# Final sums and output norm moved into the last two experts of a mixture-of-experts step, on one core

## The reference, cut to what matters

```python
h = x + mix                                     # mixer: pooling, gated linear attention, w_out
hn = rmsnorm(h, norm_ffn)
# router: the best of 4 groups, then the best 2 of its 8 experts; gates = p_group * softmax over the two
def expert_block(xb, e):                        # for the rows sent to expert e
    hid = silu(xb @ w_eg[e]) * (xb @ w_eu[e])   # 1024 -> 512
    return hid @ w_ed[e]                        # 512 -> 1024
h = h + gate1 * y(expert1) + gate2 * y(expert2)
y = rmsnorm(h, norm_final)                      # y_sample and y_prompt, without meta and padding rows
```

## Time and profile before

| what | value |
|---|---|
| median of 3 runs (lowest, highest) | 1094.62 us (1094.2, 1095.68) |
| the profiled execution | 1094.27 us, span 1092.4 us |
| PE busy | 1008.9 us, 92% of the span |
| DVE, ACT, POOL busy | 417.7, 241.8, 105.5 us |
| HBM read, written | 242.00 MB, 26.80 MB |

### The profile page before, as it was taken

How to read it: one execution, slowest core, us unless ns; L and a number is a source line. 1 busy time by engine, 2 the same in 40 slices (tenths; PEclk the granted TensorE clock), 3 DMA queues, 4 the chain that set the end, 5 groups by cost and what they waited for, 6 DMA issues and landing times.

```text
span 1092.4 us, 32850 instructions
## 1 busy us (share of the span) xinstructions
PE 1008.9 (92%) x14634; PEld 820.9 (75%) x14634; DVE 417.7 (38%) x909; ACT 241.8 (22%) x509; POOL 105.5 (10%) x168
## 2 busy tenths in 40 slices
PE   5999999999999999976999999999999999999920
PEld 5786867777686859536889888888898888988910
DVE  1433444535252535352433232232332322313338
ACT  2352222323233322130111111111111111110123
POOL 0110101010101101001101111011011110110000
PEclk9999999999999999997999999999999999999965
DMA  8900000000000000656999999999999999999557
GB/s 258 408 24 40 1 39 0 38 0 38 0 38 3 35 38 1 272 216 210 366 390 393 415 397 409 404 396 412 400 403 408 397 412 406 395 410 399 214 215 304
DMA packets 52930, 262.32 MB, mean 240 GB/s; under 512 B 10285, under 2 KB 12781, under 8 KB 44698
## 3 DMA queue, kind: packets, MB, share of 16 engines
q1 hardware_dynamic: 43130, 234.20, 54.4%
q0 software_dynamic: 7168, 18.10, 4.9%
q10 hardware_dynamic: 2592, 9.44, 2.1%
HBM read 242.00 MB, written 26.80 MB: 246 GB/s over the span
## 4 chain that ended last, share of the span: by engine, by line
PE 90%; DVE 5%; DMA 3%; ACT 1%; issue 1%; SPq 0%; ACTq 0%; POOLq 0%; DVEq 0%
PE bank L1516 32%; PE bank L1235 18%; PE bank L1356 10%; PE bank L1527 10%; PE bank L1287 6%; PE bank L1533 5%; PE bank L1223 4%; DVE arena L1201 1%; DVE arena L1199 1%; PE bank L1336 1%; DMA hn_rows<-hs 1%; DVE arena L1207 1%; DMA arena<-in_w_in 1%; PE bank L1294 1%; PE bank L1353 1%
## 5 line engine op out<-in xcount | busy, mean ns | idle before, releaser
L1235 PE MATMUL bank<-xnT,arena 128*128 128x128 f32 x1728 | 201.9, 278 | 4.8 <-DMA arena<-in_w_in 3.4
L1235 PEld LDWEIGHTS bank<-xnT,arena 128*128 128x128 f32 x1728 | 197.7, 194 | 7.5 <-DMA arena<-in_w_in 3.9
L1516 PEld LDWEIGHTS bank<-xnT,arena 128*64 128x64 f32 x4096 | 171.1, 138 | 6.6 <-issue 6.2
L1516 PEld LDWEIGHTS bank<-hnT,arena 128*64 128x64 f32 x4096 | 169.5, 137 | 7.7 <-issue 7.7
L1516 PE MATMUL bank<-xnT,arena 128*64 128x96 f32 x4096 | 174.3, 248 | 0.0
L1516 PE MATMUL bank<-hnT,arena 128*64 128x96 f32 x4096 | 172.7, 246 | 1.0 <-issue 1.0
L1083 DVE TENSOR_SCALAR mixT<-mixT 128x384 f32<-128x384 f32 x32 | 11.5, 360 | 322.8 <-ACT mixT L724 312.3
L1356 PE MATMUL bank<-arena,mixT 128*128 128x512 f32 x256 | 111.7, 593 | 0.0
L1356 PEld LDWEIGHTS bank<-arena,mixT 128*128 128x128 f32 x256 | 47.9, 190 | 57.2 <-issue 57.1
L1527 PE MATMUL bank<-arena,silu_r 128*32 128x384 f32 x768 | 85.9, 487 | 0.5 <-issue 0.5
L1533 PE MATMUL bank<-arena,silu_r 128*32 128x256 f32 x384 | 85.9, 380 | 0.0
(11 more groups left out here) (213 smaller groups left out, 956.3 us busy)
## 6 DMA issues: line engine op xcount, KB each, us to landing
arena<-in_w_eg SPq DMA_DIRECT2D x32, 2048.0 KB
arena<-in_w_eu SPq DMA_DIRECT2D x32, 2048.0 KB
arena<-in_w_ed SPq DMA_DIRECT2D x32, 2048.0 KB, 16.0
hn_rows<-hs ACTq DMA_DIRECT2D x18, 512.0 KB, 3.4
arena<-pick_rows SPq DMA_DIRECT2D x16, 512.0 KB, 10.3
arena<-in_w_in SPq DMA_DIRECT2D x3, 2048.0 KB, 14.2
arena<-in_w_out SPq DMA_DIRECT2D x1, 4096.0 KB, 24.5
out_y_prompt<-arena SPq DMA_DIRECT2D x8, 512.0 KB, 3.5
```

What stands on the lines that cost most here:

```text
L1235: last = mm(out, w_in_sb[:, k, a:b], xnT[:, k, :], start=k == 0, stop=k == KD - 1)
L1516: last = mm(out[q * SW:(q + 1) * SW, n * BLOCK:(n + 1) * BLOCK], w[:, k, m * P + q * SW:m * P + (q + 1) * SW], rowsT[b][:, k, :], start=k ...
```

## The change

**New data in DRAM.** `h_rows` gets `h` of every tile (`store_h`, on SP), `info_rows` the gates and experts of each token, `late_rows` is a second copy of the layout of `pick_rows`. Both pick tensors are first filled with `x_all` (four DRAM to DRAM transfers of 4.7 MB on SP's queue), before the first expert's rows are stored.

**Tiles early.** SP loads the tiles' two pick rows in experts 30 and 31, as soon as the pieces of `arena` are free that they go to. Tiles 0 to 2 are summed on DVE as before. Tiles 3 to 8 are summed on PE into PSUM (`pair`, two banks): 64 tokens of both picks stand stacked on 128 partitions, and a 128 x 64 matrix with two diagonals of gates (`gate_diag`) multiplies and adds both; a matmul with the identity adds `h`. Norms follow from PSUM. The tokens of experts 30 and 31 have the fill in place of such an expert's row in this pass, and are stored over below.

**Late rows by index.** For the 96 rows of each of the two last experts, POOL fetches `h`, the gates and the other pick by index; DVE sums (`late_base`, `late_sum`), ACT and DVE norm, and POOL stores the rows over the tiles' output by index, `y_sample` first, and `y_prompt` after all tiles are stored. `g_fin` (the weights of the final norm) gets a place of its own and is loaded early.

```diff
+FAR = 8192
+BY_PE = 3
+LATE = (NE - 2, NE - 1)
...
+    late_dram = nc.dram_tensor("late_rows", (PICK_ROWS, D), F32, kind="Internal").ap()
+    h_dram = nc.dram_tensor("h_rows", (ROWS, D), F32, kind="Internal").ap()
+    info_dram = nc.dram_tensor("info_rows", (P, TILES * 2 * PICKS), F32, kind="Internal").ap()
...
+        lots = [2 * i * D for i in range(TILES - 1)] + [starts["u", 1]]
+        y_pair = [arena[:, at:at + 2 * D].rearrange("p (q n) -> p q n", q=2) for at in lots]
+        gate_diag = free_work[:, D:D + (TILES - BY_PE) * P].rearrange("p (t q m) -> p t q m", q=2, m=CHUNK)
...
+        l_h = rows
+        l_sum = [free_work[0:BLOCK, 0:D], k_er[0:BLOCK, :]]
...
+            for k in range(PICKS):
+                sp.dma_start(y_dram[k * ROWS:(k + 1) * ROWS, :], x_all).then_inc(s["filled"], 16)
+                sp.dma_start(late_dram[k * ROWS:(k + 1) * ROWS, :], x_all).then_inc(s["filled"], 16)
...
+            def store_h(j):
+                if j < TILES - 1:
+                    sp.wait_ge(s["h_added"], j + 1)
+                else:
+                    sp.wait_ge(s["own_added"], 2)
+                sp.dma_start(h_dram[j * P:(j + 1) * P, :], h_all[:, j, :]).then_inc(s["h_stored"], 16)
+            for j in range(TILES - 1):
+                store_h(j)
             sp.wait_ge(s["pe_v"], TILES)
             load_weights(0, 0)
             load_weights(0, 1)
+            store_h(TILES - 1)
+            sp.dma_start(g_fin, norm_final.partition_broadcast(P)).then_inc(s["g_fin_in"], 16)
...
+            def load_tile(i):
+                for k, y in ((0, y1[i]), (1, y2[i])):
+                    at_row = k * ROWS + i * P
+                    if i < BY_PE:
+                        sp.dma_start(y[0:OUT_ROWS[i], :], y_dram[at_row:at_row + OUT_ROWS[i], :]).then_inc(y_in[i], 16)
+                    else:
+                        sp.dma_start(y_pair[i][k * CHUNK:(k + 1) * CHUNK, :, :],
+                                     y_dram[at_row:at_row + P, :].rearrange("(q m) n -> m q n", m=CHUNK)).then_inc(y_in[i], 16)
+            def store_tile(i):
+                sp.wait_ge(s["out_ready"], i + 1)
+                if i == 0:
+                    sp.dma_start(y_sample, y2[i][0:SAMPLE, :]).then_inc(s["sample_stored"], 16)
+                else:
+                    sp.dma_start(y_prompt[(i - 1) * P:i * P, :], y2[i]).then_inc(s["tiles_stored"], 16)
+            sp.wait_ge(s["pe_g"], NE - 1)
+            for b in range(2):
+                sp.wait_ge(ye_stored[b], 16 * (NE // 2 - 1))
+            load_tile(0)
+            load_tile(1)
+            sp.wait_ge(s["pe_u2"], 2 * (NE - 1))
+            load_tile(2)
+            load_tile(3)
+            sp.wait_ge(s["pe_d"], NE - 1)
+            load_tile(4)
+            load_tile(5)
+            sp.wait_ge(s["pe_g"], NE)
+            load_tile(6)
+            load_tile(7)
+            store_tile(0)
+            sp.wait_ge(s["pe_u2"], 2 * NE)
+            load_tile(8)
             sp.wait_ge(s["slots_ready"], 1)
             n_x = sp.value_load(steer[0:1, 0:1], min_val=0, max_val=EXTRA)
-            sp.wait_ge(s["pe_d"], NE)
+            for i in range(1, TILES):
+                store_tile(i)
+            sp.wait_ge(s["outs_stored"], 16 * (2 * PAIRS + 2))
+            sp.wait_ge(s["l_put"], 16 * 2 * NLATE)
...
+            pool.wait_ge(s["h_stored"], 16 * TILES)
+            pool.wait_ge(s["late_idx_ready"], 1)
+            pool.wait_ge(s["info_stored"], 16)
             for b in range(2):
-                scatter(NE // 2 - 1, b)
-
+                fetch(l_info[:, b, :], info_rows, i_late[:, 4, b:b + 1], ROWS).then_inc(s["l_info_in"], 16)
+            pool.wait_ge(s["pe_eT"], NE - 1)
+            fetch(l_h[0], h_dram, i_late[:, 0, 0:1], ROWS).then_inc(l_h_in[0], 16)
+            for b in range(2):
+                pool.wait_ge(ye_stored[b], 16 * (NE // 2 - 1))
+            for b in range(2):
+                fetch(l_sum[b], y_dram, i_late[:, 1, b:b + 1], PICK_ROWS).then_inc(l_other_in[b], 16)
+            pool.wait_ge(s["pe_eT"], NE)
+            fetch(l_h[1], h_dram, i_late[:, 0, 1:2], ROWS).then_inc(l_h_in[1], 16)
+            pool.wait_ge(s["ye_ready"], YE_STEPS * (NE - 1))
+            put(late_dram, idx_i[:, LATE[0]:LATE[0] + 1], ye[0], PICK_ROWS).then_inc(ye_stored[0], 16)
+            pool.wait_ge(ye_stored[0], 16 * (NE // 2))
+            pool.wait_ge(l_other_in[1], 16)
+            pool.wait_ge(s["late_idx_ready"], 2)
+            fetch(l_sum[1], late_dram, i_late[:, 5, 1:2], PICK_ROWS).then_inc(s["other_again"], 16)
...
+            pool.wait_ge(s["sample_stored"], 16)
+            for b in range(2):
+                pool.wait_ge(s["l_out_ready"], b + 1)
+                put(y_sample, i_late[:, 3, b:b + 1], l_h[b], SAMPLE).then_inc(s["l_put"], 16)
+            pool.wait_ge(s["tiles_stored"], 16 * (TILES - 1))
+            for b in range(2):
+                put(y_prompt, i_late[:, 2, b:b + 1], l_h[b], SEQ).then_inc(s["l_put"], 16)
...
+            t = NE // 2 - 1
+            gate(t, 0)
+            out_rows(t, 0)
+            gate(t, 1)
+            for i in range(BY_PE):
+                tile_rstd(i)
+            out_rows(t, 1)
+            tile_rstd(3)
+            late_rstd(0)
+            tile_rstd(4)
+            tile_rstd(5)
+            tile_rstd(6)
+            late_rstd(1)
+            tile_rstd(7)
+            tile_rstd(8)
...
+            dve.wait_ge(s["pe_gates"], 1)
+            for k in range(PICKS):
+                own = slice(k * CHUNK, (k + 1) * CHUNK)
+                V.tensor_copy(gate_pair[own, :, :], bank[0][own, 0:2 * NP].rearrange("p (q t k) -> p t q k", q=2, k=PICKS)[:, BY_PE:, :, k]).then_inc(s["gates_turned"], 1)
...
+            def late_base(b):
+                dve.wait_ge(l_h_in[b], 16)
+                dve.wait_ge(l_other_in[b], 16)
+                if b == 1:
+                    dve.wait_ge(s["other_again"], 16)
+                final.then(V.scalar_tensor_tensor(out=l_sum[b], in0=l_sum[b], scalar=l_gates[:, 1, b:b + 1], in1=l_h[b], op0=ALU.mult, op1=ALU.add))
+            def late_sum(b):
+                dve.wait_ge(s["ye_ready"], YE_STEPS * (LATE[b] + 1))
+                V.scalar_tensor_tensor(out=l_sum[b], in0=ye[b], scalar=l_gates[:, 0, b:b + 1], in1=l_sum[b],
+                                       op0=ALU.mult, op1=ALU.add).then_inc(s["l_sum_ready"], 1)
+            def late_out(b):
+                dve.wait_ge(s["l_rstd_ready"], b + 1)
+                V.scalar_tensor_tensor(out=l_h[b], in0=l_sum[b], scalar=l_ss[:, b:b + 1], in1=g_fin[0:BLOCK, :],
+                                       op0=ALU.mult, op1=ALU.mult).then_inc(s["l_out_ready"], 1)
+            t = NE // 2 - 1
+            expert(t, 0)
+            late_small()
+            gated(t, 1)
+            hidden(t, 1, 0)
+            combine(0)
+            hidden(t, 1, 1)
+            combine(1)
+            normalize(0)
+            combine(2)
+            normalize(1)
+            late_base(0)
+            late_sum(0)
+            normalize(2)
+            normalize(3)
+            late_out(0)
+            normalize(4)
+            normalize(5)
+            late_base(1)
+            late_sum(1)
+            normalize(6)
+            late_out(1)
+            normalize(7)
+            normalize(8)
...
+                    pe.wait_ge(s["eT_ready"], 2 * e + 2)
+                    pe.wait_ge(s["weights_done"], 1)
+                    for q in range(2):
+                        for k in range(PICKS):
+                            last_gate = mm(bank[0][k * CHUNK:(k + 1) * CHUNK, q * NP:(q + 1) * NP], ident[:, q * CHUNK:(q + 1) * CHUNK],
+                                           gate_all[:, :, :].rearrange("p t k -> p (t k)"), start=True, stop=True)
+                    last_gate.then_inc(s["pe_gates"], 1)
...
+            pe.wait_ge(s["diag_ready"], 1)
+            for i in range(BY_PE, TILES):
+                out = pair[(i - BY_PE) % 3]
+                pe.wait_ge(y_in[i], Y_IN)
+                if i >= BY_PE + 3:
+                    pe.wait_ge(s["out_ready"], i - 2)
+                for n in range(2):
+                    own = slice(n * 512, (n + 1) * 512)
+                    for q in range(2):
+                        mm(out[q * CHUNK:(q + 1) * CHUNK, own], gate_diag[:, i - BY_PE, q, :], y_pair[i][:, q, own], start=True, stop=False)
+                    for q in range(2):
+                        half_tile = slice(q * CHUNK, (q + 1) * CHUNK)
+                        last = mm(out[half_tile, own], ident[:, half_tile], h_all[:, i, own], start=False, stop=True)
+                last.then_inc(s["pe_sum"], 1)
```

More of the change, by code:

```diff
@@ L519, in _, with fetch, put @@
                     scatter(t - 1, b)
-            for b in range(2):
-                scatter(NE // 2 - 1, b)
+            def fetch(out, src, index, count):
+                return nc.gpsimd.indirect_dma_start(out, None, src, bass.IndirectOffsetOnAxis(ap=index, axis=0),
```

(38 more changed lines are left out.)

255 lines of the change are left out of this document (167 added, 88 removed).

## The result

The changed kernel takes 1112.18 us (median of six runs, 1105.97 to 1118.02), the kernel before 1095.23 beside it: 1.0148 times as long, 95% interval 1.0109 to 1.0187. The prediction said 1085.6, with a range of 1078 to 1093, and gave slower a chance of 0.11. The profiled execution took 1113.39 us, its span is 1111.6. Before, the runs lay within 0.2% of each other; now they spread over 1.1%.

What follows compares the result with a forecast made beforehand. PE bounds the expert loop; the change touches the waiting chains at both ends. Span 1092.4 - 17.0 (end) + 7.2 (front) + 0.2 + 0.6 = 1083.4; with 1.87 and 0.35 for execution and median, 1085.6 us, range 1078 to 1093.

Steps and rivals of the forecast that it cites:

- The front: From the mixer to the first expert: later first weights delay last store and gather, so PE starts 7.2 us later.
- the last store of `hn_rows`: Before the first expert: the last tile's rows meet some 11.5 more large weight packets and land 5.7 us later.
- the gather: POOL's fetch by index before the first expert: it meets 4 KB packets and takes 1.5 us more.
- the rule of the Trainium skill: DMA queues at the front: engines drain a whole packet of descriptors before switching, so the last stores end near 500.
- the count's 501.2: Front: landing of the last tile's stores if one packet of SP's queue goes between two of theirs.
- The fills: 18.9 MB of DRAM fills during the mixer: they cost nothing, or 0 to 14 us at half speed.
- the tiles' loads: Experts 30 and 31: 9 MB at 403 GB/s take some 23 us, so tiles 0 to 2 arrive in time.
- The room: Last two experts: the DMA engines are only 10% busy, leaving space for the tiles' early loads.
- The order around tile 0: Last hidden layer: tile 0's sum before the second half starts down 1.9 us later and costs nothing.
- PE's sums: End: quarter-array matmuls, 8 a tile, two at a time, take 1.7 us a tile and keep up.
- POOL's end: After tile 8's store: POOL's start, two index stores and the second's landing take 4.7 us.
- The slower rival: End: PE's sums run one by one at half clock, 6.9 us a tile, giving 1108.2 us; chance 0.05.

Runs made afterwards that it cites:

- e6_all: Changed kernel with tiles 3 to 8 loaded over 128 partitions, two `h` stores behind the first weights, tile 0's sum behind the last hidden half: 1090.47 us, ratio 0.9963.
- e3_order: Changed kernel with tile 0's sum moved behind the second half of expert 31's hidden layer: 1107.38 us, ratio 1.0134 against the kernel before.
- e9_noput: e6_all without the last two index stores of late rows into `y_prompt`: 1088.27 us, ratio 0.9939 against the kernel before.
- e7_tile0: e6_all with tile 0's two loads taking 128 rows over all partitions instead of 64: 1088.55 us, ratio 0.9937 against the kernel before.

## Why the prediction was wrong

**The front: right.** SP's first weights went out at 464.87 (predicted 465), the last store of `hn_rows` landed 4.1 us later than before (499.59 against 495.52; predicted 5.7), the gather took 4.0 more (predicted 1.5), PE's first turn came 8.1 later (predicted 7.2, at about 508). Store and gather shared the price differently. The landing, 499.59, lies nearer to what the rule of the Trainium skill gave ("DMA: Bandwidth & Descriptors", queues, rings and completion order; near 500) than to the count's 501.2; one landing does not decide it. The fills cost nothing: the mixer's length is unchanged.

**The step that failed: the tiles' loads.** "Even 9 MB take some 23 us at the loop's 403 GB/s, so tiles 0 to 2 are there in time." The rate was taken from transfers that fill 128 partitions and applied to loads into 64. They ran at 205 GB/s. Tile 0 was 6.80 us late for DVE, tile 8 landed at 1091.76. The room was read too generously as well: the 10% of the earlier trace rows begin at 1025, but the loads were issued at 1033.42, which by the kernel before's clock (8.1 + 2.2 us earlier) is 1023.1. There the last weights were still under way (share 0.65 from 1020 to 1025 in the kernel before). In the changed kernel they and the tiles' loads then ran side by side, and the last down piece landed 30.1 us after its issue.

The last norm ended 51.8 us behind the last hidden product (DVE's operation at 1046.73) where the prediction had 31.3: 20.5 us. In e6_all it is 41.4, so the rate of tiles 3 to 8, the order and the front account for half of it.

**The order around tile 0: wrong through the same step.** "That costs nothing" held for a tile that is there. As it was not, PE's last down products waited with it, and through SP's queue so did tile 8's load, issued 4.3 us earlier in e3_order.

**PE's sums: a tile mis-sized by two.** Predicted 8 matmuls of 0.43, two at a time: 1.7 us. The view of line 1870, the half of the sums with the gates:

```profile
L1870 PE MATMUL pair<-arena,gate_work x48: 592/592/1112, 1070.7 to 1094.0; 128*64 128x512 f32 x48
```

In the code these are 24 matmuls (six tiles, two halves of the columns, two of the rows): each is two records, and so were the matmuls of the earlier trace rows (288 records for 144 in the code), whose 0.43 us was the price of one record. A tile has 16 records, the chain shows four in 0.86 us at full clock, 3.43 in all. Two at a time was right. Half clock came only with the first tile's sum (granted 0.50 from 1070.70 to 1074.10), 5.6 us for that tile.

**The other half of the 20.5 us** is seen in e6_all, 41.4 us against 31.3, and the size of the sums explains it only in part. By the prediction's own numbers sums of 3.4 us a tile, started at 1045.9, would end 1.8 us after ACT wants tile 8. In e6_all six of them take 20.8 us, but they begin 17.6 us behind the last hidden product, at 1053.49, where the prediction had PE free 9.5 behind it. These 8.1 us are again the crowded DMA engines and what followed from them: the wait for the down weights (3.07 us), the half clock behind it, and the wait for tile 3 (2.10). What sums of half the size would have gained after so late a start, no run shows.

**POOL's end: left out.** Predicted 4.7 us behind the last store; it was 9.4 (1102.19 to 1111.6). Up to the landing of the second index store the prediction was right: issued at 1104.21, it landed 2.7 us later, 4.7 behind the tile's store. But it let the program end there. The drain, which lasts until 1111.33, was not in the sum, although the trace of the kernel before has it too, 5.4 us long and hidden.

**The sum again:** 20.5 for the loads with what hung on them, the order and PE's sums, 0.7 for a store of 3.67 instead of 3.0, 4.7 for POOL's end, 0.9 at the front and 1.4 in between: 28.2, the distance from 1083.4 to 1111.6. The slower rival (PE's sums one by one at half clock, 1108.2) came close in number and not in mechanism: its threshold of 4.6 us a tile was not reached.

## What to carry to other kernels

Price a transfer by the partitions that it fills on chip, not only by its bytes, and read GB/s beside the share in every window: a full share at half the rate is its own finding. Count what is still in the queues when the new transfers are issued, and what they will delay: here it was also the last weights. Spreading rows over every second partition restored the rate for the price of another constant. And when work is moved to an engine that did not finish last before, count that engine's own end.

## What the runs showed of the hardware that was not expected

- Loads into 64 neighbouring partitions: 205 to 230 GB/s at a share of 1.03 to 1.04; into every second of 128 partitions 398, into 128 407.
- POOL's drain at the end of a program with index stores: 5.4 to 7.8 us in all twelve kernels, whether its last store had landed (e9_noput, 6.03) or not.
- An fp32 matmul of the code with 512 columns is two records, 0.43 us each in the chain.
- After a wait of 5.26 us PE ran its next matmuls at a granted clock of 0.50 from 1051.28 to 1054.70 (e7_tile0), and its sums ended no earlier than in e6_all, though they began 2.2 us before.
